# Differential attention: GpSimd combines the last 256 key columns of each head's weights

## The reference

```
def _diff_attend(q, k, v, lam):
    s = jnp.einsum('bhcqd,bhckd->bhcqk', q, k, preferred_element_type=jnp.float32) * (A_DQK ** -0.5)
    p = jax.nn.softmax(s, axis=-1)
    w = p[:, :, 0] - lam * p[:, :, 1]
    return jnp.einsum('bhqk,bhkd->bhqd', w.astype(v.dtype), v)
```

## Time and profile before

| | |
|---|---|
| median of 3 executions | 3502.75 us (3502.69 to 3503.0) |
| profiled execution: its time / its span | 3500.57 / 3498.8 us |
| PE, DVE, ACT, POOL busy, share of the span | 87%, 50%, 31%, 8% |
| chain that ended last, by engine | PE 56%, issue 23%, DVE 13%, ACT 5% |
| row maxima, L1520 | 144 instructions, 197.5 us |
| exponentials, L1121 | 144 main instructions, 178.0 us |
| combine, L1538 | 72 instructions, 103.2 us |
| group copies, L1132 | 200 instructions, 97.1 us |
| latent attention, layers 1 and 2 | about 638 to 858 us and 2437 to 2660 us of the span |
| PE, DVE, ACT, POOL busy in the first of these, of 220 us | 168.57, 181.02, 148.02, 7.05 us |

### The profile page before, as it was taken

How to read it: one execution, slowest core, us unless ns; L and a number is a source line. 1 busy time by engine, 2 the same in 40 slices (tenths; PEclk the granted TensorE clock), 3 DMA queues, 4 the chain that set the end, 5 groups by cost and what they waited for, 6 DMA issues and landing times.

```text
span 3498.8 us, 45250 instructions
## 1 busy us (share of the span) xinstructions
PE 3039.4 (87%) x17454; PEld 1644.6 (47%) x17454; DVE 1745.2 (50%) x2354; ACT 1074.4 (31%) x1670; POOL 282.9 (8%) x202
## 2 busy tenths in 40 slices
PE   5897878777999999999997579678778899999997
PEld 3453644454445655555544234444554344444443
DVE  4884745786364311222235695645884563122235
ACT  5112213565354211101124311314664442111122
POOL 0400100000220000000002230000001200000001
PEclk9898779799999999999998799769999999999998
DMA  5110010111223321111111111011222232111112
GB/s 215 36 43 12 7 44 31 43 60 37 79 66 116 120 73 51 36 42 39 42 66 43 60 37 37 6 38 43 79 74 73 77 100 81 54 44 53 48 60 102
DMA packets 59452, 206.87 MB, mean 59 GB/s; under 512 B 7361, under 2 KB 8385, under 8 KB 59329
## 3 DMA queue, kind: packets, MB, share of 16 engines
q1 hardware_dynamic: 58176, 199.89, 16.9%
q10 hardware_dynamic: 1152, 5.24, 0.4%
HBM read 200.91 MB, written 4.19 MB: 59 GB/s over the span
## 4 chain that ended last, share of the span: by engine, by line
PE 56%; issue 23%; DVE 13%; ACT 5%; POOL 1%; DMA 1%; SPq 0%; POOLq 0%; DVEq 0%; ACTq 0%
PE PS L576 52%; DVE R L1674 4%; DVE wlo L1421 2%; ACT X L1095 1%; ACT R L1093 1%; DVE R L1499 1%; DVE R L1486 1%; ACT whi L1043 1%; DMA R<-in_w_ada 1%; POOL st L2036 1%; DVE R L1796 1%; PE PS L607 1%; PE PS L853 1%; DVE X L1770 0%; POOL X L1968 0%
## 5 line engine op out<-in xcount | busy, mean ns | idle before, releaser
L576 PE MATMUL PS<-R,whi 128*128 128x512 f16 (+1 forms) x7808 | 2133.1, 361 | 119.5 <-DVE wlo L1421 48.0
L576 PE MATMUL PS<-R,wlo 128*128 128x512 f16 (+1 forms) x3904 | 1406.3, 360 | 0.0
L576 PEld LDWEIGHTS PS<-R,whi 128*128 128x128 f16 x7808 | 763.2, 99 | 905.4 <-issue 75.4
L576 PEld LDWEIGHTS PS<-R,wlo 128*128 128x128 f16 x3904 | 384.8, 99 | 382.6 <-issue 17.7
L1421 DVE SCALAR_TENSOR_TENSOR wlo<-stage,whi 128x1024 f16<-128x1024 f32 (+1 forms) x260 | 332.1, 1277 | 463.5 <-ACT whi L1043 448.8
L1043 ACT ACTIVATE whi<-stage 128x1024 f16<-128x1024 f32 (+1 forms) x260 | 268.9, 1034 | 168.9 <-PE PS L576 134.9
L1968 POOL TENSOR_TENSOR X<-X 128x512 f32<-128x512 f32 (+1 forms) x98 | 135.5, 1386 | 1713.0 <-ACT X L1342 1591.7
L1674 DVE SCALAR_TENSOR_TENSOR R<-X,small,R 128x1024 f32<-128x1024 f32 (+1 forms) x180 | 219.0, 1266 | 1.8
L1520 DVE TENSOR_REDUCE tiny<-PS 128x1 f32<-128x1280 f32 (+1 forms) x144 | 197.5, 1371 | 30.1 <-PE PS L667 26.8
L1908 DVE SCALAR_TENSOR_TENSOR X<-X,PS 128x512 f32<-128x512 f32 (+3 forms) x60 | 62.0, 1034 | 295.9 <-PE PS L576 295.8
L1903 DVE SCALAR_TENSOR_TENSOR X<-X,PS 128x512 f32<-128x512 f32 (+3 forms) x60 | 62.1, 1035 | 292.2 <-ACT X L1359 292.2
(11 more groups left out here) (190 smaller groups left out, 2252.3 us busy)
## 6 DMA issues: line engine op xcount, KB each, us to landing
stage<-in_w_gu SPq DMA_DIRECT2D x120, 512.0 KB, 3.4
X<-in_w_ada SPq DMA_DIRECT2D x60, 512.0 KB, 3.4
stage<-in_w_down SPq DMA_DIRECT2D x48, 512.0 KB, 3.5
stage<-in_w_in SPq DMA_DIRECT2D x44, 512.0 KB, 3.5
stage<-in_w_out SPq DMA_DIRECT2D x32, 512.0 KB, 3.5
T<-in_w_ada SPq DMA_DIRECT2D x20, 512.0 KB, 3.5
R<-in_w_ada SPq DMA_DIRECT2D x16, 512.0 KB, 12.0
stage<-in_w_down SPq DMA_DIRECT2D x16, 384.0 KB, 3.0
```

The lines of the kernel that those rows point to most:

```text
L576: last = mm(slot(j, t0, t1)[:, c0 - t0:c1 - t0], w[:, j, k, :], row, start=(k == 0 and q == 0), stop=(k == K - 1 and q == 2))
```

## The change

In latent runs DVE combines columns 0 to 1023 alone. GpSimd does columns 1024 to 1279, the third group's 256, in two instructions with a wait between them: `w = P2 * beta`, then `w = w + P1`. `beta` goes from one shared column to one of two by head parity, with a semaphore `beta`; GpSimd counts its finished heads in `w_end`. PE's turn of the third group, ACT's exponentials and DVE's next use of a `beta` column wait for `w_end`. On DVE one reciprocal of both sums replaces the scaling of d1 and the reciprocal of d2, and the tile's last reciprocal becomes a multiplication of four columns.

```diff
-                    d1, d2 = den[:, h % 2, 0:1], den[:, h % 2, 1:2]
-                    TS(rl[:, h:h + 1], d1, XS, None, ALU.mult)
-                    own.link(nc.vector.reciprocal(beta[:, 1:2], d2))
-                    own.link(STT(beta[:, 0:1], d1, lamv[:, 10 + l:11 + l], beta[:, 1:2], ALU.mult, ALU.mult))
+                    own.link(nc.vector.reciprocal(rec[:, h, :], den[:, h % 2, :]))
+                    share = beta[:, h % 2:h % 2 + 1]
+                    if not (isinstance(r, int) and n < 2) and NG == 3:
+
+                        dve.wait_ge(s("w_end"), n - 1)
+                    STT(share, den[:, h % 2, 0:1], lamv[:, 10 + l:11 + l], rec[:, h, 1:2],
+                        ALU.mult, ALU.mult).then_inc(s("beta"), 1)
+                    dve.wait_ge(s("beta"), n + 1)
                     if not (isinstance(r, int) and n < 2):
 
                         dve.wait_ge(s("wt_ps"), NG * n - NG)
-                    STT(Wt[h % 2][:, 0:keys], P2[h % 2][:, 0:keys], beta[:, 0:1], P1[h % 2][:, 0:keys],
+                    mine = min(keys, POOL_KEY)
+                    STT(Wt[h % 2][:, 0:mine], P2[h % 2][:, 0:mine], share, P1[h % 2][:, 0:mine],
                         ALU.mult, ALU.add).then_inc(s("w"), 1)
                     if h == HA - 1:
-                        own.link(nc.vector.reciprocal(rinv[:, :], rl[:, :]))
+                        own.link(TS(rinv, rec[:, :, 0], 1.0 / XS, None, ALU.mult))
...
                         pe.wait_ge(s("exps"), 2 * n + 4 if not (isinstance(r, int) and n == 4 * nt - 1) else 2 * n + 2)
+                        pe.wait_ge(s("w_end"), n + 1)
...
                         act.wait_ge(s("w"), n - 1)
+                        if NG == 3:
+                            act.wait_ge(s("w_end"), n - 1)
...
+                    def last_keys(r, h):
+
+                        n = 4 * r + h
+                        pool.wait_ge(s("beta"), n + 1)
+                        if not (isinstance(r, int) and n < 2):
+
+                            pool.wait_ge(s("wt_ps"), NG * n - NG)
+                        w, p1, p2 = (b[h % 2][:, POOL_KEY:keys] for b in (Wt, P1, P2))
+                        own.link(TT(w, p2, beta[:, h % 2:h % 2 + 1].to_broadcast([P, keys - POOL_KEY]), ALU.mult))
+                        TT(w, w, p1, ALU.add).then_inc(s("w_end"), 1)
...
+                    def tile(r, first=False):
+                        for h in range(HA):
+                            if h == 3 and not first:
+                                inverse(r - 1)
+                            if h or not first:
+                                last_keys(*back(r, h, 1))
```

More of the change, by code:

```diff
@@ L153, in build @@
         st8 = sb("st8", [P, 4, 8])
-        rl, rinv = st8[:, 3, 0:4], st8[:, 3, 4:8]
+        rec, rinv = st8[:, 3, 0:8].rearrange("p (h c) -> p h c", c=2), st8[:, 2, 4:8]
         PS = ctx.enter_context(nc.psum_tensor("PS", [P, 8, 512], F32))
@@ L260, in build @@
             for run in (("c", "l") if l < LAYERS - 1 else ("l",)):
-                for n in "scores nbias exps w wt_ps wt pv pv_out".split():
+                for n in "scores nbias exps w wt_ps wt pv pv_out beta w_end".split():
                     S[f"{n}_{run}{l}"] = sem(f"{n}_{run}_{l}")
@@ L397, in back @@
             return (r, h - n) if h >= n else (r - 1, HA + h - n)
+        POOL_KEY = 1024
         ADA_FIRST = 2 * KD
@@ L1577, in tile @@
                         maxima(r, h, 1)
-                per = 8 + 8 + 1 + 2
+                per = 8 + 4 + 1 + 2
                 tile(0, first=True)
@@ L2037, in _, with inverse @@
                 for run, t_first, nt, nk in attend_runs(l):
-                    done = tiles_before(l, run)
-                    with pool.Fori(0, nt) as r:
+                    done, keys, NG = tiles_before(l, run), nk * P, len(key_groups(nk))
+                    s = lambda n: S[f"{n}_{run}{l}"]
+                    def last_keys(r, h):
[6 more added lines that the diff above has]
+                        TT(w, w, p1, ALU.add).then_inc(s("w_end"), 1)
+                    def inverse(r):
                         pool.wait_ge(S["o_var"], r + (done + 1))
@@ L2042, in _ @@
                            ALU.pow).then_inc(S["o_pow"], 1)
+                    if keys <= POOL_KEY:
+                        with pool.Fori(0, nt) as r:
+                            inverse(r)
+                        continue
+                    def tile(r, first=False):
[4 more added lines that the diff above has]
+                                last_keys(*back(r, h, 1))
+                    tile(0, first=True)
+                    with pool.Fori(1, nt) as r:
+                        own.enter(r - 1, HA)
+                        tile(r)
+                    own.leave(nt - 1, HA)
+                    last_keys(nt - 1, HA - 1)
+                    inverse(nt - 1)
                 k1, k3 = step_of(4 * l + 1, 0), step_of(4 * l + 3, 0)
```

## The result

Over 20 executions each, the changed kernel takes 3507.33 us (3504.19 to 3509.49) and the kernel before 3501.57 (3497.12 to 3503.0). The ratio is 1.0018, with a 95% interval of 1.0012 to 1.0024: slower by 5.8 us, at the edge of what can be told from no change. That is 2.3 us above the forecast of 3505 and inside its range. The profiled execution has a span of 3505.6 us, where that of before had 3498.8.

A forecast was written before the change was run, and what follows sets the result against it. At tile boundaries PE's list, started by head 2's combine, was taken to bound: one combine in four counts. 2.9 us lost there less 0.5 in the context run made +2.4, 3505 on the shown median 3502.75; range 3493 to 3512.

The forecast's parts named there:

- DVE stands still until GpSimd's instruction is over, and ends 1.08 after it: Two-input SBUF instructions on DVE and GpSimd take turns; a 1024-column DVE one ends 1.08 us after GpSimd's.
- GpSimd first: At each latent head's `beta`, GpSimd starts 0.03 us earlier and goes ahead of the combine; likeliest case, 3503 to 3509.5, chance 0.40.
- The combine's end: In latent heads, the combine ends 1.88 us after `beta`, against 1.69 before: 0.19 us later.
- DVE first: Rival: the combine gets in ahead of GpSimd's multiply, ending 0.33 us earlier at the boundary; 3497 to 3499.5, chance 0.33.
- the dearer collision: Rival: GpSimd's broadcast multiply is slower than an add, delaying boundary and middle heads; 8 to 10 us, 3514, chance 0.12.
- What GpSimd first costs a tile: Per latent tile, the later combine costs 0.18 us, between 0.05 and 0.45; 16 tiles pay 2.9 us.
- the middle heads: Heads inside a tile: combine 0.23 us late, just held by the maximum's slack; PE's slack leaves perhaps 0.05 us.
- The combine of the last head, ahead of the 0.45 us gap: At a tile's last head, a later combine was to cost nothing, since DVE's next maximum waits 0.45 us for PE.
- No wait for `w_end`: PE, ACT and DVE waits for GpSimd's share taken at zero; they would cost from about 5.5 us after `beta` on.
- The context run's gain of 0.5 us: Context run, without a GpSimd share: 8 heads gain 0.06 us each from fewer small instructions, 0.5 us.
- TensorE's clock: Rival: shifted waits remove clock drops in half the tiles (3490, chance 0.10) or add some (3512, chance 0.05).
- the clock gives back: Rival: in half of the 16 tiles TensorE's clock drop disappears, gaining 13 us: 3490, chance 0.10.

The follow-up runs named there:

- a reciprocal at the end: Changed kernel with the four-column multiplication at the tile's end replaced by a reciprocal of the same four columns: 3501.97 us, 1.0005 of before.
- the three kernels without the hold-up: Changed kernel with the tile's last multiplication made a reciprocal (1.0005 of before), moved ahead of `beta` (1.0011), or split into four one-column ones (1.0013).
- GpSimd after DVE: Changed kernel with GpSimd's multiply waiting for `w`, the end of DVE's combine, in place of `beta`: 3494.09 us, 0.9982 of before.
- DVE released sooner: Changed kernel with DVE's `wt_ps` wait ahead of the reciprocal and the four-column multiplication ahead of `beta`; GpSimd still waits for `beta`: 3496.79 us, 0.9986 of before.
- the inverse early: Changed kernel with the four-column multiplication put ahead of the `beta` instruction of the tile's last head: 3502.16 us, 1.0011 of before.

## Why the prediction was right, and where its sizes were off

**DVE stands still until GpSimd's instruction is over, and ends 1.08 after it: shown.** In the changed kernel it ends 1.08 us after the multiply in all 64 heads, and taking turns gives back all of the combine's 0.44 us. Two readings of the earlier trace rows need a word. The row taken for "alone" (111.55) stands inside GpSimd's add of 110.39 to 115.03, which was waiting; 1.23 us is still the undisturbed length, which most instructions of that line have. And the add waited there until 112.78, for two DVE instructions one after the other: this one and one of L1674 that started at 110.36 and took its undisturbed 1.28. So the turns needn't alternate.

**GpSimd first: right, but the reason given was wrong.** The step "I take it that the earlier one goes first, which is GpSimd by 0.03 us" failed. In the looped tiles GpSimd started 0.17 to 0.19 us after `beta` (taken: 0.11). In 63 of all 64 heads it was behind DVE, by 0.03 to 0.05, and it went first in each. Had I known the starts, this rule would have given "DVE first", 3497 to 3499.5. That the order came out as forecast was luck. "Nothing in the trace shows so close a start" was wrong as well: the instruction at 110.36 just named started 0.03 us ahead of GpSimd's add, and there DVE went first.

**The combine's end: 1.86 to 1.87 us after `beta` in 55 heads, taken 1.88.** Two errors cancel: the start was 0.06 later than taken, the multiply 0.08 shorter (0.61 for 0.69). The wait at the boundary shown grew by 0.11, taken 0.13. This also answers the dearer collision: it needed a multiply longer than an add, and at 0.61 us it is shorter than the add's 0.73.

**What GpSimd first costs a tile: 0.18 taken, about 0.045 measured.** The kernel with a reciprocal at the end has this cost alone: 27.25 / 27.30 against 27.19 / 27.27, 0.06 and 0.03 more. The step that was off is the middle heads', which were taken to add 0.05. In a regular tile of layer 2, the times from the combine of head 2 to that of head 3 and on to the next tile's first are 0.08 and 0.04 us longer than before, about the 0.13 of the sum, but the next head is 0.09 shorter (5.78 for 5.87): it gives most of it back.

**The combine of the last head, ahead of the 0.45 us gap, was taken to cost nothing: this term was mis-sized.** The combine's own 0.19 does fit into the gap, but the four-column multiplication behind it is held up by GpSimd's add for 0.53 us, in all 16 tiles. I had named such a hold-up only under DVE first, and with the multiply. Together they fill the gap, and the maximum is late. From the last head's combine to the next tile's first, a regular tile of layer 2 now takes 6.60 us, before 6.10 and with a reciprocal at the end 6.14; the next two heads (5.67 and 8.42 us, with a reciprocal 5.78 and 8.54) give half of it back. So a middle head isn't "unchanged" at 5.9 us either.

The price is the difference to the kernel with a reciprocal at the end: 27.32 less 27.25 = 0.07 us a tile in layer 1 and 27.53 less 27.30 = 0.23 in layer 2; with 8 tiles each that makes 2.4 us. So regular tiles make 16 x 0.045 + 2.4 = 3.1 us, where the forecast had 2.9. The medians of the three kernels without the hold-up, 1.0005, 1.0011 and 1.0013, lie under 1.0018 as this asks, but their intervals overlap with its own. The fastest of 11 executions is 3500.35 to 3500.67 in each of the three; the fastest of the changed kernel's 20 is 3504.19.

**No wait for `w_end`: right.** Neither the page nor the chain has PE or ACT waiting for the add; the kernel that leaves GpSimd's share out is no faster than GpSimd after DVE.

**The context run's gain of 0.5 us** was 0.3 at most: from the first to the last of its combines the changed kernel and six of its variants take 21.2 us, four variants 21.3 to 21.4, the kernel before 21.45. In the whole time neither this nor the small instructions can be told from nothing.

**The total: 2.4 us slower forecast, 5.8 measured.** That 3505 looks nearer to 3507.33 than this is luck: the forecast stood on the three executions shown, 3502.75, and over 20 that kernel takes 3501.57. About 3.1 us of the 5.8 are accounted for by the regular tiles; for the other 2.7 no cause is shown.

**TensorE's clock** was a rival. Between the two profiled executions it takes part: of the 6.8 us, the seven tiles of layer 2 have 4.6, of which the four regular ones have 1.1, while the seven of layer 1 have -0.1; the rest lies at the ends of the runs and outside attention. But on average the change didn't lower the clock: it is 0.9225 over the 20 executions of the changed kernel and 0.9226 over 87 of the kernel before (0.9229, 0.9222 and 0.9229 in its three series). A mean doesn't tell where in a tile the clock fell, so the rival isn't excluded for the other 2.7 us, but a lower clock isn't what explains them. For the faster kernels it is different. Where the combine takes 1.28 us or less the mean clock is 0.9234 to 0.9250, in all others 0.9217 to 0.9238. So the rival "the clock gives back" came true in part there: of the 7.6 us by which GpSimd after DVE beats the kernel before, 5.2 are in regular tiles (0.30 and 0.35).

**DVE first** was priced at 3497 to 3499.5. As a kernel of its own (DVE released sooner, with the inverse early as well) it measured 3496.79 beside a before of 3501.4: 4.6 us faster, where the rival's parts make 3.4 to 5.8. A regular tile is 0.40 / 0.39 us shorter, more than the 0.18 to 0.33 of the rival, but several tiles of this kernel are 1 us longer than its regular ones.

## What to carry to other kernels

When GpSimd takes a share of a DVE instruction, don't release both by one semaphore: with rows of SBUF on both sides the two took turns here, so the parallel work wasn't parallel, and who goes first is decided by hundredths of a microsecond. Let GpSimd wait for DVE's result if its deadline allows it, put it beside instructions of DVE that it can't disturb (here the maximum from PSUM, 1.49 us beside GpSimd and alone), and look at every small DVE instruction in its shadow. Before any of this, leave the share out once: that run is the most that the split can bring, here 0.19%.

## What the hardware did that I had not expected

**The one that starts later by the profile can go first.** GpSimd's multiply went first whenever it started up to 0.045 us behind DVE's combine (all cases, seven kernels). At 0.047 to 0.049 behind, it did so once, and DVE went first in four kernels' one case each. From 0.12 behind on DVE always went first. This holds for this pair of instructions, both released after a wait; with the add of 1324 columns, 0.034 us behind a DVE instruction in a row of others (110.36 and 110.39, before), DVE went first. These are the starts that the profile records; whether GpSimd asks for its rows before its recorded start, or DVE after its own, no row shows. The edge, on the timeline of the kernel with a reciprocal at the end:

```profile
660.14 1.28 DVE L1547 SCALAR_TENSOR_TENSOR R<-R,tiny 128x1024 f32<-128x1024 f32 x1
...
660.19 1.71 POOL L2058 TENSOR_TENSOR R<-R,tiny 128x256 f32<-128x256 f32 x1 [3.75 <-DVE tiny L1540]
```

**A one-input DVE instruction can be held up as well, depending on its form.** Four columns multiplied by a constant: 0.69 us beside GpSimd's add, 0.164 alone. One column: 0.14 to 0.15 beside it. A reciprocal of four: 0.164. The Trainium skill has a rule for it. Its page GPSIMD Engine Reference (section Specifications) says that GpSimd contends with DVE instructions with two SBUF inputs or in a 2-port mode. By the Trainium skill's page VectorE: DVE Perf Modes (Mode 2×_2P), a multiplication by a constant can take that mode, which needs source and destination in SBUF and their outermost dimension longer than one even, or odd and equal. Four columns held up and one column let through agree with this; that the mode was in use no row here shows. I had read the two pages only for the two-input case. Of a reciprocal neither of these sections says anything, so that it is let through is this case's measurement alone.

**GpSimd on 128 partitions of fp32.** Undisturbed, a multiply by a broadcast column takes 0.40, 0.61 and 1.04 us for 128, 256 and 512 columns, an add of two rows 0.45, 0.73 and 1.27.
